# A two-layer SwiGLU trunk on one core: the FFN unit in K halves, and a stage's ninth out slab around its last unit

## The reference

```python
def swiglu_ffn(x, w_in, w_out):
    gate, up = jnp.split(x @ w_in, 2, axis=-1)
    return (jax.nn.silu(gate) * up) @ w_out
...
for i in range(DEPTH):                                # DEPTH = 2
    x = x + 0.5 * swiglu_ffn(rms_norm(x, ffn1_norm[i]), ffn1_w_in[i], ffn1_w_out[i])
    xn = rms_norm(x, mix_norm[i])
    # i = 0: causal pooling and a gated depthwise convolution between two projections
    # i = 1: spatial gating between two projections
    x = x + y
    x = x + 0.5 * swiglu_ffn(rms_norm(x, ffn2_norm[i]), ffn2_w_in[i], ffn2_w_out[i])
return rms_norm(x, final_norm)
```

## Time and profile before

| what | value |
|---|---|
| median of 3 runs | 942.45 us |
| profiled execution, its own time | 941.8 us |
| its span | 940.1 us |
| PE busy | 920.0 us, 98% |
| DVE, ACT busy | 524.8 us, 422.0 us |
| share of the chain that ended last | PE 87%, DMA 4%, DVE 3%, issue 3%, ACT 2% |
| HBM read | 168.63 MB |

### The profile page before, as it was taken

One profiled execution on the slowest core, in us unless ns is written; L12 is line 12 of the kernel. 1 busy time (PEld: TensorE's weight loads), 2 busy tenths in 40 slices (PEclk: granted clock), 3 DMA queues, 4 the chain that ended last, 5 costly groups with the idle time before them and its releaser, 6 DMA issues.

```text
span 940.1 us, 11406 instructions
## 1 busy us (share of the span) xinstructions
PE 920.0 (98%) x4361; PEld 765.9 (81%) x4361; DVE 524.8 (56%) x505; ACT 422.0 (45%) x458; POOL 29.8 (3%) x44
## 2 busy tenths in 40 slices
PE   8999999999999899999999999999999989999997
PEld 7788888888887688888887888888899868888885
DVE  5755445546967645445457454454578475454533
ACT  6544344336844544343445443434464264443422
POOL 1600000000000000000000000000010000000000
PEclk9999999999999999999999999999999999999999
DMA  8874655523413955666518656465184286566411
GB/s 282 293 265 142 216 179 201 180 90 135 157 46 121 309 196 175 209 219 232 179 59 294 199 178 211 148 227 183 60 296 151 90 266 230 176 198 203 158 44 45
DMA packets 126668, 170.20 MB, mean 181 GB/s; under 512 B 5237, under 2 KB 111241, under 8 KB 126632
## 3 DMA queue, kind: packets, MB, share of 16 engines
q1 hardware_dynamic: 126632, 169.70, 53.9%
HBM read 168.63 MB, written 1.05 MB: 180 GB/s over the span
## 4 chain that ended last, share of the span: by engine, by line
PE 87%; DMA 4%; DVE 3%; issue 3%; ACT 2%; SPq 0%; POOL 0%; DVEq 0%; POOLq 0%; ACTq 0%
PE acc L962 10%; PE acc L964 10%; PE acc L963 10%; PE ga L962 9%; PE ga L964 9%; PE ga L963 9%; PE ub L962 8%; PE ub L964 8%; PE ub L963 8%; DMA raw<-in_ffn_w_out_dram 3%; DVE w_lo L669 2%; PE tp L1066 2%; ACT w_hi L454 2%; PE ga L1186 1%; PE tp L1023 1%
## 5 line engine op out<-in xcount | busy, mean ns | idle before, releaser
L669 DVE TENSOR_TENSOR w_lo<-raw,w_hi 128x2048 fp32r<-128x2048 f32 (+1 forms) x154 | 351.3, 2285 | 253.1 <-ACT w_hi L454 253.1
L454 ACT ACTIVATE w_hi<-raw 128x2048 fp32r<-128x2048 f32 (+1 forms) x154 | 293.7, 1909 | 213.8 <-PE acc L964 94.3
L962 PE MATMUL acc<-w_hi,act_hi 128*128 128x512 f32 x416 | 163.8, 394 | 2.5 <-DVE act_lo L764 2.5
L964 PE MATMUL acc<-w_hi,act_lo 128*128 128x512 f32 x416 | 162.1, 390 | 0.0
L963 PE MATMUL acc<-w_lo,act_hi 128*128 128x512 f32 x416 | 161.9, 389 | 0.0
L962 PE MATMUL ga<-w_hi,xn_hi 128*128 128x512 f32 x384 | 151.2, 394 | 3.2 <-DVE sgh L758 2.8
L962 PE MATMUL ub<-w_hi,xn_hi 128*128 128x512 f32 x384 | 153.6, 400 | 0.0
L964 PE MATMUL ub<-w_hi,xn_lo 128*128 128x512 f32 x384 | 150.1, 391 | 0.0
L964 PE MATMUL ga<-w_hi,xn_lo 128*128 128x512 f32 x384 | 149.7, 390 | 0.0
L963 PE MATMUL ub<-w_lo,xn_hi 128*128 128x512 f32 x384 | 149.7, 390 | 0.0
L963 PE MATMUL ga<-w_lo,xn_hi 128*128 128x512 f32 x384 | 149.5, 389 | 0.0
(11 more groups left out here) (133 smaller groups left out, 615.4 us busy)
## 6 DMA issues: line engine op xcount, KB each, us to landing
raw<-in_ffn_w_in_dram SPq DMA_DIRECT2D x176, 512.0 KB, 4.9
raw<-in_ffn_w_out_dram SPq DMA_DIRECT2D x88, 512.0 KB, 4.1
raw<-in_sgu_w_in_dram SPq DMA_DIRECT2D x16, 512.0 KB, 4.4
raw<-in_ab_w_in_dram SPq DMA_DIRECT2D x12, 512.0 KB, 4.7
raw<-in_ab_w_out_dram SPq DMA_DIRECT2D x8, 512.0 KB, 3.8
raw<-in_sgu_w_out_dram SPq DMA_DIRECT2D x8, 512.0 KB, 5.8
gain<-in_ffn_norm_dram SPq DMA_DIRECT2D x4, 512.0 KB, 5.7
xres<-in_x_dram SPq DMA_DIRECT2D x2, 512.0 KB, 5.9
```

The source lines that it names most:

```text
L454: act.activation(w_hi[:, n % RING, o:], raw[:, n % RAW, o:], ACT.Copy).then_inc(hi_split, 1)
L669: dve.tensor_tensor(w_lo[:, n % RING, o:], raw[:, n % RAW, o:], w_hi[:, n % RING, o:].bitcast(F32), ALU.subtract).then_inc(lo_split, 1)
L962: pe.matmul(dst, s_hi, m_hi, start=start, stop=False)
L964: return pe.matmul(dst, s_lo, m_hi, start=False, stop=stop)
```

## The change

`unit` takes both token tiles of the first K half, then the transposes of the unit before, then both tiles of the second half; so slab n is used up in the middle of the unit instead of at three quarters, and row 0 is full at three quarters instead of in the middle. The wait for `ub_free` comes 12 matmuls earlier than before, counted from the start of the unit. ACT and DVE handle the hidden part and the split of slab n+6 first, and then row 0's gate and product, right ahead of row 1's. At the start of a stage only the split of b+4, no longer that of b+5, stands between the gates of row 0 and row 1. The ninth out slab of a stage leaves `tail`: its token tile 0 comes between units 9 and 10, and its tile 1 between unit 10 and the last transposes. `first_unit` and `tail` itself are otherwise as before, and so are the number of instructions and all loads.

```diff
 # ACT, FFN stage
                     gate_rows(0, b, r, f, ACT.Silu)
-                    split_to(b + 5)
+                    split_to(b + 4)
                     gate_rows(1, b, r, f, ACT.Silu)
                     split_to(b + 7)
                     with act.Fori(0, (STEPS - 3) // 2) as i:
                         for j in range(2):
                             n, s = b + 2 + 3 * j, 1 + j
-                            gate_rows(0, n, r + s, f + s, ACT.Silu, i)
                             hidden_hi(j, j, e + j, i)
                             split(n + 6, i)
+                            gate_rows(0, n, r + s, f + s, ACT.Silu, i)
                             gate_rows(1, n, r + s, f + s, ACT.Silu, i)
                             split(n + 7, i)
                             split(n + 8, i)
...
 # DVE, the same places: product_rows for gate_rows, hidden_lo for hidden_hi
...
 # PE, unit
                 pe.wait_ge(ga_free, at(f, 2, i))
                 rows_in(n, 0, 0)
+                pe.wait_ge(ub_free, at(f, 2, i))
+                rows_in(n, 1, 0).then_inc(slab_used, 1)
+                if between is not None:
+                    between()
                 slab_ready(n + 1, i)
                 rows_in(n + 1, 0, 1).then_inc(first_rows, 1)
-                pe.wait_ge(ub_free, at(f, 2, i))
-                if between is not None:
-                    between()
-                rows_in(n, 1, 0).then_inc(slab_used, 1)
                 rows_in(n + 1, 1, 1).then_inc(slab_used, 1)
...
 # PE, end of an FFN stage
                     n = b + 2 + 3 * (STEPS - 3)
-                    for s in (STEPS - 2, STEPS - 1):
-                        unit(n, f + s, None, lambda: turned_late(s))
-                        n += 2
-
-                    def last_turned():
-                        pe.wait_ge(ga_free, f + STEPS)
-                        pe.wait_ge(ub_free, f + STEPS)
-                        turned(tp[0])
-
-                    tail(k, [(n + a, 2 * a) for a in range(3)],
-                         lambda a: pe.wait_ge(h_done, e + STEPS - 2 + a), None, last_turned)
+                    out8 = n + 4
+
+                    def eighth(t):
+
+                        slab_ready(out8)
+                        pe.wait_ge(h_done, e + STEPS - 2)
+                        return slab_out(out8, t, 0, False, False)
+
+                    unit(n, f + STEPS - 2, None, lambda: turned_late(STEPS - 2))
+                    eighth(0)
+                    unit(n + 2, f + STEPS - 1, None, lambda: turned_late(STEPS - 1))
+                    eighth(1).then_inc(slab_used, 1)
+
+                    pe.wait_ge(ga_free, f + STEPS)
+                    pe.wait_ge(ub_free, f + STEPS)
+                    turned(tp[0])
+                    tail(k, [(out8 + a, 2 * a) for a in (1, 2)],
+                         lambda a: pe.wait_ge(h_done, e + STEPS - 1 + a))
```

More of the change, by code:

```diff
@@ L540, in _ @@
                     for s in (STEPS - 2, STEPS - 1):
-                        gate_rows(0, n, r + s, f + s, ACT.Silu)
                         hidden_hi((s - 1) % 2, (s - 1) % 2, e + s - 1)
                         split_to(n + 6)
+                        gate_rows(0, n, r + s, f + s, ACT.Silu)
                         gate_rows(1, n, r + s, f + s, ACT.Silu)
@@ L796, in _ @@
                             n, s = b + 2 + 3 * j, 1 + j
-                            product_rows(0, g + 2 * s, e + s, i)
                             hidden_lo(j, j, e + j, i)
                             split(n + 6, i)
+                            product_rows(0, g + 2 * s, e + s, i)
                             product_rows(1, g + 2 * s, e + s, i)
@@ L819, in _ @@
                     for s in (STEPS - 2, STEPS - 1):
-                        product_rows(0, g + 2 * s, e + s)
                         hidden_lo((s - 1) % 2, (s - 1) % 2, e + s - 1)
                         split_to(n + 6)
+                        product_rows(0, g + 2 * s, e + s)
                         product_rows(1, g + 2 * s)
@@ L1087, in full_in, with tail @@
                 slab_in(n, open_bank(n, which, f, i, per)).then_inc(slab_used, 1)
-            def tail(k, slabs, ready, start=None, late=None):
+            def tail(k, slabs, ready, start=None):
                 for t in range(TT):
@@ L1094, in tail @@
                         last = a == len(slabs) - 1
-                        if t == 0 and a == 1 and late is not None:
-                            late()
                         if t == 0:
```

## The result

Both kernels were timed in 20 executions each: 944.45 us median after (941.68 to 947.17), 941.87 us before (940.36 to 944.64). The ratio is 1.0024, with a 95% interval of 1.0013 to 1.0035. So the change makes the kernel slower by a quarter per cent: 2.6 us where +0.2 was forecast. The median lies 0.05 us above the stated range (941.0 to 944.4 us), and the ratio just outside the "no change" within 0.2% that was called likeliest. The profiled execution after took 942.7 us with a span of 940.9 us, only 0.8 us more than before: it is one of the better ones.

What follows compares the result with a forecast made beforehand. TensorE was taken to bound the kernel, busy 920.0 of 940.1 us at full clock. Terms -0.33 - 0.33 + 0.80 - 0.16 - 0.50 + 0.72 = +0.20 us on 942.45 gave 942.6 us, range 941.0 to 944.4.

Steps and rivals of the forecast that it cites:

- no change: Whole kernel: the forecast itself, no measurable difference, within 0.2% or 1.9 us; chance 0.70.
- What bounds the kernel: Whole kernel: TensorE busy 920.0 of 940.1 us at full clock, loop at its floor, some 20 us winnable at most.
- 80 new joins: Loop: two new joins from ga to ub per unit, 0 to 0.11 us each, taken as 0.
- The waits that move: Stage starts: the wait before the transposes reappears before the out slab, about 2.9 us in the third stage, gaining 0.33 us.
- The new wait in the first stage: First stage, before unit 2: row 0's product now stands behind the split of b+8, +0.80 us.
- Mixer 0: Mixer 0's pool unit: 12 matmuls of row 1 now cover the gaps between the K halves, -0.50 us.
- The ninth out slab: Ends of three FFN stages: fewer matmuls cover token tile 0's norm, 0.24 us each, +0.72 us.
- Third and fourth stage: Their starts: hidden part comes ahead of row 0's product but stays behind the split of b+7, -0.33 us each.
- the prediction's own sign of being wrong: Starts' out slabs over 1 us earlier than before after subtracting earlier shifts, or a loop distance other than 16.8 us.
- Sixth stage: Its start: row 0's product behind the split of b+8 cuts the gain of 0.33 us to -0.16 us.
- Sum at full clock: Whole kernel: all terms together +0.20 us, with no term for the clock.
- the clock rival: New joins or third stage's joined wait: PE falls to 1.2 GHz, 5.5 us each time, 948 us for one; chance 0.03.

Runs made afterwards that it cites:

- r1: The changed kernel again with no edit: 943.87 us, ratio 1.0013 to the kernel before.
- r5: The kernel before again with no edit: 943.03 us, ratio 0.9993.
- r3: The kernel before with only the ninth out slab in two parts around the last unit: 943.27 us, ratio 1.0011.
- r9: The kernel before with only row 1's gate and product of the first unit ahead of the split of b+5: 946.25 us, ratio 1.0027.
- r4: The kernel before with the new unit order and ACT and DVE order, last three out slabs together in the tail: 942.26 us, ratio 1.0008.
- r11: Changed kernel with old tail, hidden part one split earlier, and row 0's first gate and product before b+3's split in FFN stages two to four: 935.10 us.
- r6: The changed kernel with 7 small matmuls in the wait before the first out slab of the third and sixth stage: 943.93 us, ratio 1.0012.

## Why the prediction was right, and where not

- **What bounds the kernel: right.** The loop keeps its 16.80 us, unit for unit, and all that happened lies at stage starts and ends. The 80 new joins cost nothing: in the changed kernel ga and ub follow each other at 0.22 us, with the wait on `ub_free` between them:

```profile
231.28 0.39 PE L964 MATMUL ga<-w_hi,xn_lo 128*128 128x512 f32 x1
231.50 0.39 PE L962 MATMUL ub<-w_hi,xn_hi 128*128 128x512 f32 x1
```

- **The waits that move: right in place, their sizes less so.** The prediction has the 1.98 us wait reappear before the out slab, joined with the 0.95 us there: it did, but as 1.96 us in the third stage, and the sixth has one of 2.28 us. The 2.9 us named for it does not fit its own sum, which takes 0.33 us off and so leaves 2.6; the load took off the rest. The new wait in the first stage was priced at 0.80 us and measured 0.81 (45.08 to 45.89). That close a hit is in part luck: unit 2 starts at 46.70 in r1 and at 46.19 in r5, 0.5 us apart.
- **Mixer 0: right.** The offset to before falls from +1.19 to +0.59 us over it, so 0.60 us won for 0.50 forecast.
- **The ninth out slab: right.** The transposes and the stage's next matmul, for the earlier trace rows:

```profile
479.86 1.28 PE L1023 MATMUL tp<-ident,xs 128*128 128x128 f32 x8
480.90 0.48 PE L962 MATMUL acc<-w_hi,act_hi 128*128 128x512 f32 x1
```

  1.04 us instead of 0.79, in three places 0.21 to 0.25 us; r3 measures the part alone at +0.9 us for 0.72. The list of waits doesn't show it as waits before L1023, as was foretold; it shows as a longer group.
- **Third and fourth stage: mechanism right, size off.** 1.2 and 0.8 us were won for 0.33 each in the one pair of profiles. In the third stage this trips the prediction's own sign of being wrong, an out slab more than 1 us earlier after earlier shifts: 319.13 before, 317.95 after. The split of b+7 starts 0.85 us earlier against unit 1, because its load landed earlier. Loads vary by about 1 us from one execution to the next (in r5 the first out slab of the first stage starts 1.1 us later than in the earlier trace rows), which the sum took as fixed. But that is not all of it. From unit 1's start to the out slab of the third stage it is 14.76, 14.27 and 14.47 us in the three profiles with the old order (before, r5, r3) and 13.58, 13.82 and 13.81 with the new one, a mean gain of 0.8 us; in the fourth stage the mean gain is 0.6. "Nothing here starts earlier" was wrong by 0.3 to 0.4 us a stage, and no run shows why.
- **Sixth stage: mechanism right, size not measured.** For -0.16 us the one pair of profiles shows +0.3, the clock's 1.6 us aside. Over three profiles of each order the difference is 0.1 us, with 0.4 us of scatter.
- **Sum at full clock: right within the noise, in part by luck.** +0.2 us forecast, -0.4 us measured, to about 0.6 us. In the one pair of profiles the third and fourth stage won 1.3 us more than their terms and the sixth 0.5 less, so errors cancel in part. That the median of 944.45 us lies within 0.05 us of the range is luck too: the sum has no term for the clock, which made the kernel slower, and by the difference to before it is 2.6 us instead of 0.2.
- **The failed step: the clock rival and its chance.** The text gave "PE's clock falls to 1.2 GHz, at the new joins or in the joined wait" 0.03, against it "the clock is full through 1.98 us of waiting", with 5.5 us for one. It is what happened. The joined wait was named beside the joins, and it was the wait: r9 has it without the joins. The price was too high by a factor of three: 1.6 us each time, as the clock is back before the out slab ends. The chance was far too low: a wait of 1.98 us without effect says little of one of 2.3 to 2.9, and the argument took one execution's trace for all. The changed kernel had a clock of 0.997 or less in 23 of 32 executions.
- The Trainium skill's rule on cycling through banks ("TensorE: Matmul & The Clock Gate", section "A second HAM failure mode: psum-queue depth-cycling") was weighed for the joins. The trace doesn't agree with it here: with 80 more joins the loops keep their 16.80 us, and in the changed kernel's profile only the stretch behind a wait of 2.28 us has a lower clock before the last matmul.

## What to carry to other kernels

Moving a wait away from one place is worth nothing if what is awaited stays behind the same load: follow the awaited result through its engine's queue, and move that. Two short waits joined into one can cost more than they did apart, because the matmuls behind the longer one may run at half speed; and one profile may not show it (r4's doesn't), while the granted clock of many executions does. Putting the small step that PE needs ahead of a split whose slab PE needs only after another out slab and another unit was, on top of the change, worth 1% against the kernel before, ten times as much as any term of the change.

## What the hardware showed

- Behind waits of PE of up to 1.98 us no lower clock was seen in the profiles; behind 2.00 (r11), 2.07 (r6), 2.25 (r1), 2.28 and 2.59 us it fell some matmuls on, behind 4.10 us it was low at the first. But behind 2.17 (r4) and 2.18 us (r1, third stage) it stayed at full speed. So the length of the wait alone does not decide it between 2.0 and 2.2 us. Matmuls then start 0.43 us apart instead of 0.23, and one such stretch cost 1.6 us.
- A 128x128 matmul of plain float32 operands is two records and 0.235 us here (14 calls, 28 records, 3.29 us).
